# Modulations in six units, decay products of 256 and 384 columns, fixed PSUM banks in the second block's norms

## The reference, cut to what matters

```
silu_c, silu_cc = jax.nn.silu(c), jax.nn.silu(c_ctx)
for l in range(DEPTH):
    mod = (silu_c @ w_ada[l] + b_ada[l])[:, None, :]
    sh1, sc1, g1, sh2, sc2, g2 = jnp.split(mod, 6, axis=-1)
    ...
    x = _post(x, _latent_mixer(_modulate(x, sh1, sc1), mem, ...), g1, ...)
    x = _post(x, _ffn(_modulate(x, sh2, sc2), p), g2, ...)

# _modulate(x, shift, scale) = _layernorm(x) * (1 + scale) + shift
# _post(x, f, gate, g, b)    = _layernorm(ALPHA * x + gate * f, g, b)

# gated linear attention, one chunk of 64 tokens (_gla_scan)
b = jnp.cumsum(gc, axis=2)
a = jnp.einsum('bhid,bhjd,bhijd->bhij', qc, kc, jnp.exp(b_i - b_j))   # i >= j
o = (q * exp(b)) @ state + a @ v
```

```
h = rms_norm(x, attn_pre_norm[l]);  x = x + rms_norm(mixer(h), attn_post_norm[l])
h = rms_norm(x, ffn_pre_norm[l]);   x = x + rms_norm(conv_ffn(h), ffn_post_norm[l])
```

## Time and profile before

| | us |
|---|---|
| runs | 3023.43, 3025.18, 3025.1 |
| median | 3025.1 |
| the profiled execution | 3023.75 |
| its span | 3021.9 |

### The profile page before, as it was taken

How to read it: one execution, slowest core, us unless ns; L and a number is a source line. 1 busy time by engine, 2 the same in 40 slices (tenths; PEclk the granted TensorE clock), 3 DMA queues, 4 the chain that set the end, 5 groups by cost and what they waited for, 6 DMA issues and landing times.

```text
span 3021.9 us, 45542 instructions
## 1 busy us (share of the span) xinstructions
PE 2827.2 (94%) x19100; PEld 2426.8 (80%) x19100; DVE 1323.3 (44%) x2717; ACT 1314.7 (44%) x2204; POOL 1382.4 (46%) x646
## 2 busy tenths in 40 slices
PE   7999998899999999998999998999997899888998
PEld 5778876688876788887778798989986799776898
DVE  3777767532233211005686754232237442175440
ACT  3254433323524322225464345454454565445563
POOL 3432030234441533434532266768762488532786
PEclk9999999999999999999999999999999999899999
DMA  6332022133334343335321144446543255432454
GB/s 236 120 105 81 29 77 63 56 119 92 108 100 171 113 146 119 119 98 184 105 63 31 54 146 136 152 129 181 179 123 115 84 182 177 122 105 98 137 181 122
DMA packets 103555, 359.50 MB, mean 119 GB/s; under 512 B 11126, under 2 KB 17526, under 8 KB 102840
## 3 DMA queue, kind: packets, MB, share of 16 engines
q1 hardware_dynamic: 103352, 356.60, 37.1%
HBM read 355.51 MB, written 1.05 MB: 118 GB/s over the span
## 4 chain that ended last, share of the span: by engine, by line
PE 78%; DVE 11%; ACT 7%; POOL 3%; issue 1%; DMA 1%; SPq 0%; DVEq 0%; ACTq 0%
PE PS L357 78%; POOL RINGL L2504 2%; DVE AR L1787 2%; ACT AR L1155 2%; ACT WH L1135 1%; ACT AR L1682 1%; DVE AR L1791 1%; ACT L1155 1%; DVE PS L1795 1%; DVE SM L1787 1%; ACT XT L1155 1%; DVE SM L2021 1%; DVE XT L1787 1%; DVE AR L2388 1%; DVE HT L1787 1%
## 5 line engine op out<-in xcount | busy, mean ns | idle before, releaser
L2504 POOL TENSOR_TENSOR RINGL<-RING,WH 128x1024 fp32r<-128x1024 f32 (+1 forms) x554 | 1300.6, 2360 | 1529.0 <-ACT WH L1135 1528.4
L357 PE MATMUL PS<-HTR,WH 128*128 128x256 f32 (+2 forms) x2736 | 875.8, 321 | 0.0
L1135 ACT ACTIVATE WH<-RING 128x1024 fp32r<-128x1024 f32 (+1 forms) x554 | 568.7, 1035 | 651.8 <-PE PS L357 523.7
L357 PE MATMUL PS<-HTH,WH 128*128 128x256 f32 (+1 forms) x2336 | 748.2, 322 | 28.0 <-POOL RINGL L2504 22.7
L357 PE MATMUL PS<-HTH,RINGL 128*128 128x256 f32 (+1 forms) x2336 | 726.9, 317 | 4.1 <-POOL RINGL L2504 4.1
L357 PE MATMUL PS<-ARR,WH 128*128 128x256 f32 (+2 forms) x2688 | 690.9, 325 | 17.5 <-ACT WH L1135 5.8
L357 PEld LDWEIGHTS PS<-HTR,WH 128*128 128x128 f32 (+1 forms) x2736 | 523.9, 191 | 40.2 <-issue 2.1
L357 PEld LDWEIGHTS PS<-ARR,WH 128*128 128x128 f32 (+1 forms) x2688 | 466.7, 191 | 63.8 <-issue 15.9
L357 PEld LDWEIGHTS PS<-HTH,WH 128*128 128x128 f32 x2336 | 448.9, 192 | 70.1 <-issue 29.4
L357 PEld LDWEIGHTS PS<-HTH,RINGL 128*128 128x128 f32 x2336 | 444.7, 192 | 33.5 <-POOL RINGL L2504 5.3
L357 PE MATMUL PS<-ARR,RINGL 128*128 128x256 f32 (+1 forms) x1472 | 466.3, 327 | 1.5 <-POOL RINGL L2504 1.5
(11 more groups left out here) (195 smaller groups left out, 3437.5 us busy)
## 6 DMA issues: line engine op xcount, KB each, us to landing
RING<-w_ada_in SPq DMA_DIRECT2D x96, 512.0 KB, 3.7
RING<-w_up_in SPq DMA_DIRECT2D x88, 512.0 KB, 3.3
RING<-w_gates_in SPq DMA_DIRECT2D x48, 512.0 KB, 3.6
RING<-w_ff_gate_in SPq DMA_DIRECT2D x44, 512.0 KB, 3.8
RING<-w_ff_up_in SPq DMA_DIRECT2D x44, 512.0 KB, 3.7
RING<-w_glu_in SPq DMA_DIRECT2D x32, 512.0 KB, 4.5
RING<-w_ff_down_in SPq DMA_DIRECT2D x32, 512.0 KB, 3.5
RING<-w_in_in SPq DMA_DIRECT2D x32, 512.0 KB, 3.6
```

What stands on the lines that cost most here:

```text
L357: return e.matmul(out_, lhsT, rhs, start=start, stop=stop)
L1135: e.activation(RINGS[name][:, j, 0:width], RING[:, b % NSLOT, 0:width], ACT.Copy).then_inc(*a_upper.up(b))
L2504: e.tensor_tensor(RINGL[:, i, 0:width], RING[:, i, 0:width], RINGS[name][:, j, 0:width], ALU.subtract).then_inc(*g_lower.up(b))
```

## The change

1. **Modulations.** The 24 groups become quarters of six units. A quarter takes the same 4 blocks (with the weights stored in another order), but they are the products of two of the eight feature slices with 1024 output columns, so that four quarters add up in one PSUM bank (`start` in the first, `stop` in the last). Row copy, turn and addition of the bias come once for each unit: 4 products of 8 columns (`PICK`) on PE. They stand at the second quarter of the next unit (ACT: at the first). The bank is 6, for unit 4 it is 7.
2. **Boundary.** `fill_all` moves from between the norms into the norm `("m", 1, 1)`, on PE behind the spreading of 1/deviation, on ACT behind the root, on DVE behind the whole of `modulate`.
3. **Decay products.** `SUMS` is read as 256 columns, two pieces of 128 with a gap of 128 between them: 4 products a tile. `EX` has 13 matrices instead of 14; the pieces are 448, 448, 384 and 384 columns wide. The one left out is the k side of the last pair, for which `grams` reads k itself (`KG`). DVE's product with k is 128 x 768.
4. **Second block's norms.** `rms` always uses bank 7, `rrstd` bank 5, `hum` bank 4, and the turn of `take` is set to 0 behind each norm.

```diff
-        SUMS = [ZR[:, 4608 + 128 * i:4736 + 128 * i] for i in range(4)]
+        LEVELS = ((0, 448), (448, 896), (896, 1280), (1280, 1664))
+        SUMS = ZR[:, 4608:5120].rearrange("p (e d n) -> p d e n", e=2, d=2)
...
             def ada_rows(a):
-                l, g = a // 12, a % 12
-                o = bank(6 + a % 2 if a < 4 or a >= 12 else 6, "ada", a, until=(a_ada, "row", a))
+                u = a // 4
+                if a % 4 == 0:
+                    bank(7 if u == 4 else 6, "ada", u, until=(a_ada, "row", u))
+                o = ps("ada", u)
                 pe.wait_ge(*a_ada.to("silu"))
-                for q in range(4):
-                    n, w, _ = load(A["w_ada"][l, 4 * g + q, :, :], 1024, False)
-                    for j in range(2):
-                        c = 64 * (q % 2) + 32 * j
-                        t = mm(o[c:c + 32, :], SCP[:, 2 * q + j, :], w[:, 512 * j:512 * j + 512], q < 2, q >= 2)
-                    t.then_inc(*p_block.up(n))
-                p_block.also("ada", a)
+                for k in (2 * (a % 4), 2 * (a % 4) + 1):
+                    for half in range(2):
+                        n, w, _ = load(A["w_ada"][u // 3, 16 * (u % 3) + 2 * k + half, :, :], 1024, False)
+                        for j in range(2):
+                            c = 64 * half + 32 * j
+                            t = mm(o[c:c + 32, :], SCP[:, k, :], w[:, 512 * j:512 * j + 512], k == 0, k == 7)
+                        t.then_inc(*p_block.up(n))
+                if a % 4 == 3:
+                    p_block.also("ada", u)
...
-                    t = mm(o[:, 2 * j:2 * j + 2], ROW[a % 2][:, 128 * j:128 * j + 128], FOLD2, True, True)
+                    t = mm(o[:, 8 * j:8 * j + 8], ROW[u % 2][:, 128 * j:128 * j + 128], PICK, True, True)
...
                     if a < hi:
-                        if a - 2 >= lo:
-                            ada_turn(a - 2)
+                        if a % 4 == 1 and a - 1 > lo:
+                            ada_turn(a // 4 - 1)
                         ada_rows(a)
...
             def fill_all():
                 fill(100)
-                ada_turn(ada_at[2] - 2)
-                ada_turn(ada_at[2] - 1)
+                ada_turn(ada_at[2] // 4 - 1)
...
                 out_of_strips(o, RSTD, n).then_inc(*p_norm.up("rstd", *nid))
+                if nid == ("m", 1, 1):
+                    fill_all()
                 if nid[0] == "m" and nid[1:] != (0, 1):
...
-                        for i, m in enumerate(SUMS):
-                            g = 2 * tile + i % 2
-                            mm(o[:, i * P:i * P + P], LU[n % 2][:, g, :], m, True, False)
-                            t = mm(o[:, i * P:i * P + P], LL[seq][:, g, h * P:h * P + P], m, False, True)
+                        for d in range(2):
+                            g = 2 * tile + d
+                            mm(o[:, d], LU[n % 2][:, g, :], SUMS[:, d], True, False)
+                            t = mm(o[:, d], LL[seq][:, g, h * P:h * P + P], SUMS[:, d], False, True)
...
-                    for c in range(4):
-                        o = take("level", u, c, l, until=(a_gla, "level", l, u, c))[:, 0:448]
+                    for c, (a, b) in enumerate(LEVELS):
+                        o = take("level", u, c, l, until=(a_gla, "level", l, u, c))[:, 0:b - a]
...
-                    for i in range(4, 7):
+                    for i in range(4, 6):
                         mm(b2[:, (i - 4) * P:(i - 3) * P], ex[:, 7 + i, :], ex[:, i, :], True, True)
+                    mm(b2[:, 256:384], KG[:, h, c], ex[:, 6, :], True, True)
...
                 if not last:
-                    fill_all()
                     ring("WH0")
                     layernorm(("m", l + 1, 1), XT, lambda k: pe.wait_ge(*a_norm.to("post", l, 2, k)), BOTH)
 
             def normed(nid, ready):
-                o = take("rms", *nid, until=(a_norm, "rsd", *nid))
-                hum(3 if nid == (0, 1) else 5)
+                o = bank(7, "rms", *nid, until=(a_norm, "rsd", *nid))
+                hum(3 if nid == (0, 1) else 5, 4)
...
-                o = take("rrstd", *nid, until=(d_norm, "nmul", *nid, 7))
+                o = bank(5, "rrstd", *nid, until=(d_norm, "nmul", *nid, 7))
...
-                hum(7 if nid[1] == 1 else 5)
+                hum(7 if nid[1] == 1 else 5, 4)
+                turn[0] = 0
...
-                if a >= 2:
-                    act.wait_ge(*p_ada.to("turn", a - 2))
-                copy(ROW[a % 2], ps("ada", a)).then_inc(*a_ada.up("row", a))
+                if u >= 2:
+                    act.wait_ge(*p_ada.to("turn", u - 2))
+                copy(ROW[u % 2], ps("ada", u)).then_inc(*a_ada.up("row", u))
...
-                        if a - 1 >= lo:
-                            ada_row(a - 1)
+                        if a % 4 == 0 and a > lo:
+                            ada_row(a // 4 - 1)
...
-                    tt(ex[:, 7:14, :], ex[:, 7:14, :], bc(k, 1, 7), ALU.mult).then_inc(*d_gla.up("exk", l, u))
+                    tt(ex[:, 7:13, :], ex[:, 7:13, :], bc(k, 1, 6), ALU.mult).then_inc(*d_gla.up("exk", l, u))
...
                 if not last:
+                    modulate(("m", 1, 1), BOTH, 0, 1)
                     fill_all()
-                    modulate(("m", 1, 1), BOTH, 0, 1)
```

More of the change, by code:

```diff
@@ L212, in program @@
         ATB = [view(19456 + 512 * i, 2, 256) for i in range(2)]
-        EX = [view(1792 * i, 14, 128, MGF) for i in range(2)]
+        EX = [view(1792 * i, 13, 128, MGF) for i in range(2)]
+        LEVELS = ((0, 448), (448, 896), (896, 1280), (1280, 1664))
         KW = view(17920, 4, 512)
@@ L357, in mm, with hum @@
                 return e.matmul(out_, lhsT, rhs, start=start, stop=stop)
-            def hum(n):
-                i = turn[0] % in_turn[0]
+            def hum(n, i=None):
+                i = turn[0] % in_turn[0] if i is None else i
                 if i in held:
@@ L1204, in modulate @@
                     layernorm(nid, HT, cols, done, then)
-                act.wait_ge(*d_ada.to("one", 12 * l + 2 * scale + 1))
+                act.wait_ge(*d_ada.to("one", 3 * l + scale // 2))
                 p, c = norm_parts(nid, cols)[0]
@@ L1795, in stt, with ada_mod @@
                 return e.scalar_tensor_tensor(out=out_, in0=a, scalar=s, in1=b, op0=op0, op1=op1)
-            def ada_mod(a):
-                l, g = a // 12, a % 12
-                dve.wait_ge(*p_ada.to("turn", a))
-                c = COL_AT["b_ada", l] + 4 * g
-                m = MOD[:, l, 4 * g:4 * g + 4, :]
-                tt(m, ps("ada_turn", a)[:, 0:8].rearrange("p (c n) -> p c n", n=2), bc(COL[:, c:c + 4], 2, 2),
-                   ALU.add).then_inc(*d_ada.up("mod", a))
-                if g // 2 in (1, 4):
-                    dve.wait_ge(*d_ada.to("mod", a))
-                    ts(m, m, 1.0, None, ALU.add).then_inc(*d_ada.up("one", a))
+            def ada_mod(u):
+                l, c = u // 3, 16 * (u % 3)
+                b = COL_AT["b_ada", l] + c
+                dve.wait_ge(*p_ada.to("turn", u))
+                tt(MOD[:, l, c:c + 16, :].rearrange("p (i j) n -> p i j n", i=4),
+                   ps("ada_turn", u)[:, 0:32].rearrange("p (j i n) -> p i j n", i=4, n=2),
+                   bc(COL[:, b:b + 16].rearrange("p (i j) -> p i j", i=4), 3, 2), ALU.add).then_inc(
+                       *d_ada.up("mod", u))
+                scales = {0: 8, 2: 32}.get(u % 3)
+                if scales is not None:
+                    m = MOD[:, l, scales:scales + 8, :]
+                    dve.wait_ge(*d_ada.to("mod", u))
+                    ts(m, m, 1.0, None, ALU.add).then_inc(*d_ada.up("one", u))
             def fill(n):
@@ L1811, in fill @@
                     if a < hi:
-                        if a - 2 >= lo:
-                            ada_mod(a - 2)
+                        if a % 4 == 1 and a - 1 > lo:
+                            ada_mod(a // 4 - 1)
                         ada_at[0] += 1
```

45 lines of the change are left out of this document (23 added, 22 removed).

## The result

| | before | changed |
|---|---|---|
| runs | 3023.43, 3025.18, 3025.1, 3031.34 | 3000.14, 3006.85, 3002.75, 3003.82 |
| median | 3025.14 | 3003.28 |
| profiled execution, span | 3023.75, 3021.9 | 3000.14, 2998.3 |

Ratio 0.9924, 95% interval 0.9906 to 0.9942: 21.9 us less between the medians, where 38.6 were forecast. The changed kernel was timed again on another chip (experiment 7): 3008.24 us (median of 5) against 3023.88, ratio 0.9948 [0.9935, 0.996]. Both times lie above the range that was given (2978 to 2998). All that follows compares trace with trace, 3000.14 with 3023.75, so 23.6 us.

What follows compares the result with a forecast made beforehand. TensorE (PE), busy with products for 94% of the span, was taken as the bound. Decay products 11.6, modulations 12.5, boundary 4.4 and fixed banks 10.1 sum to 38.6 us, 3025.1 to 2986.5 us; range 2978 to 2998.

Steps and rivals of the forecast that it cites:

- the part on the boundary: Between layer 0 and layer 1: moving the last group lets DVE start 4.4 us earlier, bounds 3.5 and 6.9.
- Modulations: Feature groups staying in one PSUM bank, 24 turns becoming 6: 12.5 us less over many places, bounds 7 and 14.5.
- Decay products: Decay stages of both layers: wider sums and smaller levels give 11.6 us less, bounds 8 and 15.
- The pitches: Decay products on PE, start to start: 256 columns 0.12 us, 384 columns about 0.175 us.
- the loss in the first heads: First head of each layer: levels wait for ScalarE's rounded constants, so the sums' 0.83 us are lost, 1.7 in both.
- DVE's share: Late decay heads: PE waits for DVE's predicated copies, losing 0.30 us a head in six heads, 1.8 us.
- rival C: Clock: two more stretches of some 10 us at half clock cost up to 5 us each, 2996.5 us; chance 0.12.
- Rival B: DVE binds the whole decay stage, so only 3.2 us come out there, 2994.9 us; chance 0.08.
- Fixed banks: Norm opening layer 1 of the second block: fillers meet no busy bank, 10.1 us less, bounds 9 and 10.7.
- Rival D: Second block's norms: fillers waited for data, so fixed banks leave the 10.1 us in place, 2996.6 us; chance 0.05.
- E: Attention: reset turn makes scores take a bank whose softmax isn't read yet, slower, 3034 at 0.85 us a round; chance 0.02.
- Rival A: Decay sums: merging into 256-column products gives nothing, so 6.5 us of the stage go, 2993.0 us; chance 0.11.

Runs made afterwards that it cites:

- experiment 7: The changed kernel unedited, timed again on another chip beside the kernel before: 3008.24 us, ratio 0.9948.
- experiment 1: Changed kernel with ScalarE's early rounding at the first layer-1 norm reaching six blocks ahead instead of two: 2993.33 us, ratio 0.989.
- Experiment 10: Changed kernel, rounding mended, last modulation group one step later, third group at the start ahead of the 1/deviation spreading: 2987.1 us, ratio 0.9881.
- experiment 4: Kernel before with the decay products alone (256-column sums, 13 matrices in pieces of 448, 448, 384, 384): 3018.12 us, ratio 0.9978.
- experiment 6: Kernel before with the modulations in six units alone, last turn at its old place between the norms: 3014.24 us, ratio 0.9968.

## Why the prediction was wrong

**The step that failed** is a half-sentence in the part on the boundary: the new row copy sits "between the root and three rounding copies of ScalarE, where about 0.8 us was free". It took it for granted that those copies stay at the root. Every instruction of the moved `fill_all` was counted except what it does to a count on ScalarE: its four loads changed which blocks stand first in the ring's part, and the copies came 9.6 us behind the root instead of 0.3. Instead of -4.4 us the boundary gave +7.0, an error of 11.4 us out of 15.0. Of it 8.0 are the late rounding, shown by experiment 1, and 3.0 are longer waits for modulation blocks in the last norm (3.21 us, 0.23 before). With the rounding mended the boundary has -3.9, and DVE's subtraction the 4.4 us that the section had worked out.

**Modulations**, 12.5 forecast. The trace has 17.1 us ahead of the boundary, less 6.7 for the decay stage: 10.4. Where a turn stood amid dense work it came out about as forecast: 2.6 us in the feed-forward (3.2), 1.1 and 1.0 us at the attentions (0.8 and 1.2), 0.8 behind the merge, 1.1 within the decay stage. It failed at the start, where the prediction has 1.0 us of gain and the trace 1.0 of loss; its lower bound there, 0, left that out. Two turns (2.0 us) are gone ahead of the last two blocks, but these land at 36.24 and 38.59 us, before at 36.76 and 38.02: PE waits for them in the turns' place. Experiment 10 shows this cause for the start: free the ring's places earlier, and the wait goes. In three places (start, the norm behind the mixer, the last norm) PE waits 5.8 us more for blocks than before; 3.0 of them, in the last norm, stand in the boundary's row. There the cause stays open. The same loads, issued within 1 us of their place in the norm before, took longer to land (the last two 8.5 us, 5.5 before), and experiment 4, with all turns in place, has such a wait too:

```profile
1367.04 1.37 PE L358 MATMUL PS<-RING,SCP 128*32 128x512 f32 x4 [2.40 <-DMA RING<-w_ada_in]
```

**Decay products**, 11.6 forecast, 9.3 in the trace (6.7 + 2.6). The pitches were right (0.12, 0.18), and so was the loss in the first heads (PE's wait for the rounded constants grew from 0.75 to 1.54 us in each layer, 1.6 in all, 1.7 forecast). DVE's share was mis-sized: 1.8 us lost, 0.30 in each of six heads, where PE's waits for the copies grew by 3.0 us (6.7 to 9.7), 0.97 of it in one head. Another 1.2 us are not accounted for. Two slips of the working changed little: it names eight late heads, one of them counted already as a first head, and takes six; and a seventh of 1.086 us is 0.155, not 0.135, while the measured 954 ns of the smaller product give 0.132. Timed alone the part has 6.1 us [ratio 0.9969 to 0.9986, 4 to 9 us], under the trace of the changed kernel; a stretch at half clock behind the new wait is one reason. That is a piece of rival C inside the decay stage, where the prediction did not look for it. **Rival B** falls all the same: it gave 3.2 us.

**Fixed banks**: right, 9.5 us in the trace and 8.0 timed alone against 10.1. Rival D falls, and with it E: between 1633.38 and 2592.80, where the turn's reset changes the banks of every product, the difference moves from -12.8 to -13.5 us.

**Rival A** falls. The row of the 128-column products had the answer, and the sums alone bring 0.7 to 0.9 us in most heads. The Trainium skill ("TensorE: Matmul & The Clock Gate", Part 2, step by step) says that throughput is purely the number of columns; the measurement differs: eight products of 128 and four of 256 columns have the same columns, and at 0.11 and 0.12 us from start to start they take 0.9 and 0.5 us.

**Rival C** is there at the boundary: in the 60 us from the last norm's first product on the granted clock is 0.80 in the changed kernel (0.86 in the repetition), 0.91 before and 0.94 with the rounding mended: it goes when the late rounding goes. For the whole kernel it is open: the mean granted clock rose from 0.976 to 0.980 in the first trace and was 0.976 in the repetition.

The range was too narrow since the rivals spoke of the removed work, the clock and the banks, and none of the order of work on ScalarE, where the diff moves one call. No rival gave more than 2998 except E.

## What to carry to other kernels

When loads are moved past a marker, look for everything that counts from that marker, on all engines: here a look-ahead of three blocks on ScalarE silently became a look-ahead of none and cost 8 us, and a number in one line brought 10 us back by the medians (3003.28 and 2993.33). Before removing an instruction, ask what was landing behind it: at the start of this kernel the blocks came by DMA through a ring of few places, and the time saved on PE turned into waiting, until the places were freed earlier. And compare two traces by the distance between equal instructions, place by place, before forming any theory.

## What the runs showed of the hardware

Two executions of one kernel differ in their time at half clock. The changed kernel's two traces have a mean granted clock of 0.980 at 3000 us and of 0.976 at 3008 us. Most stretches stand in the same places and last differently: the granted clock is 0.88 and 0.63 in 36:50 and again in 469:483, 0.83 and 0.66 in 565:575. One stands in a single trace: 1.00 and 0.53 in 1450:1457. So effects of 3 us and less are better read from a distance in the trace than from a handful of times, and even that distance varies: from the last norm to layer 1 it is 51.47 and 49.91 us in these two traces.

The same DMA of 512 KB in the same place lands with up to 3 us of difference. The last two modulation blocks of layer 0's last norm took 5.5 us from issue to landing (median of the two) in the kernel before, 7.0 in experiment 6, 7.5 in experiment 4, 8.3 in experiment 7 and 8.5 in the changed kernel. No run shows why.
